# Moving the head-norm sums of the input stage behind the third chunk of a later unit

## The reference, cut to what matters

```python
u = rmsnorm(h, mix_norm[l])
(fq, fk, fv, ff, dq, dk, dv, iq, ik, iw, mq, g) = jnp.split(u @ w_in[l], SPLIT_POINTS, axis=-1)
fq = rmsnorm(fq.reshape(B, S, FOX_HEADS, FOX_HEAD_DIM), fox_q_norm[l])      # fk alike
dq = rope(rmsnorm(dq.reshape(B, S, DSA_HEADS, DSA_HEAD_DIM), dsa_q_norm[l]), cos, sin)   # dk alike
iq = rope(iq.reshape(B, S, IDX_HEADS, IDX_DIM), cos_i, sin_i)               # ik alike, no norm
km = rmsnorm(km.reshape(B, M, MEM_HEADS, MEM_HEAD_DIM), mem_k_norm[l])      # mq alike
gates = jax.nn.sigmoid(g.reshape(B, S, N_BRANCHES, D))
```

## Time and profile before

| what | value |
|---|---|
| timed runs | 1811.56, 1811.9, 1815.14 us (median 1811.9) |
| profiled execution | 1814.24 us, span 1812.4 us |
| PE busy | 1770.3 us, 98% of the span |
| DVE, ACT, POOL busy | 695.6, 695.5, 816.3 us (38%, 38%, 45%) |
| granted PE clock | 0.995 over the span |
| chain that ended last | PE 90%, DVE 6%, ACT 2% |
| from unit 2's products to the scores | 392.88 to 582.58 us after the span's start |

### The profile page before, as it was taken

The page is one execution under the profiler, slowest core; times in us unless marked ns, Lnnn a source line. Parts: engine busy times, 40 slices in busy tenths (PEclk is TensorE's granted clock), DMA queues, the critical chain, the costliest instruction groups (busy, mean ns, idle before and its releaser), DMA issues.

```text
span 1812.4 us, 23268 instructions
## 1 busy us (share of the span) xinstructions
PE 1770.3 (98%) x8458; PEld 1436.1 (79%) x8458; DVE 695.6 (38%) x1129; ACT 695.5 (38%) x1117; POOL 816.3 (45%) x376
## 2 busy tenths in 40 slices
PE   7999999999999999999999999999999999999997
PEld 5888888877887777787878888888866788888886
DVE  4222240068777875235352222200675522222002
ACT  4232222155555477785342223311424432232212
POOL 4444444447565532324544444444533444444442
PEclk9999999999999999999999999999999999999998
DMA  4233232332333221112223223223251222232232
GB/s 159 93 101 96 93 102 96 100 104 84 104 115 111 70 71 48 47 47 76 99 83 103 93 94 103 93 95 102 92 147 59 93 93 93 93 103 93 93 104 70
DMA packets 49342, 168.22 MB, mean 93 GB/s; under 512 B 6008, under 2 KB 6520, under 8 KB 49152
## 3 DMA queue, kind: packets, MB, share of 16 engines
q1 hardware_dynamic: 46368, 161.86, 27.5%
q10 hardware_dynamic: 2912, 5.52, 1.0%
HBM read 161.84 MB, written 2.11 MB: 90 GB/s over the span
## 4 chain that ended last, share of the span: by engine, by line
PE 90%; DVE 6%; ACT 2%; DMA 1%; issue 1%; POOL 0%; SPq 0%; DVEq 0%; ACTq 0%
PE bank L476 25%; PE bank L478 25%; PE bank L477 25%; PE bank L671 8%; DVE input_low L1295 2%; PE bank L716 2%; PE bank L742 2%; PE bank L839 1%; PE bank L733 1%; DVE bank L1431 1%; DMA raw_weights<-weights 1%; DVE residual L1331 1%; PE bank L545 0%; ACT weights_high L939 0%; DMA residual<-x_t 0%
## 5 line engine op out<-in xcount | busy, mean ns | idle before, releaser
L409 POOL TENSOR_TENSOR weights_low<-raw_weights,weights_high 128x1024 fp32r<-128x1024 f32 x296 | 717.7, 2426 | 934.2 <-ACT weights_high L939 933.9
L476 PE MATMUL bank<-input_high,weights_high 128*128 128x512 f32 x1424 | 560.3, 393 | 15.9 <-DVE input_low L1295 15.2
L477 PE MATMUL bank<-input_high,weights_low 128*128 128x512 f32 x1424 | 556.4, 391 | 0.0
L478 PE MATMUL bank<-input_low,weights_high 128*128 128x512 f32 x1424 | 556.1, 391 | 0.0
L939 ACT CAST weights_high<-raw_weights 128x1024 fp32r<-128x1024 f32 x296 | 308.2, 1044 | 307.4 <-DMA raw_weights<-weights 289.9
L476 PEld LDWEIGHTS bank<-input_high,weights_high 128*128 128x128 f32 x1424 | 268.4, 189 | 78.9 <-issue 12.5
L478 PEld LDWEIGHTS bank<-input_low,weights_high 128*128 128x128 f32 x1424 | 268.5, 189 | 56.6
L477 PEld LDWEIGHTS bank<-input_high,weights_low 128*128 128x128 f32 x1424 | 268.7, 189 | 55.0 <-issue 0.2
L478 PE MATMUL bank<-hidden_low,weights_high 128*128 (+1 forms) x528 | 205.5, 389 | 0.0
L476 PE MATMUL bank<-hidden_high,weights_high 128*128 (+1 forms) x528 | 205.5, 389 | 0.0
L477 PE MATMUL bank<-hidden_high,weights_low 128*128 (+1 forms) x528 | 205.5, 389 | 0.0
(11 more groups left out here) (237 smaller groups left out, 1842.1 us busy)
## 6 DMA issues: line engine op xcount, KB each, us to landing
raw_weights<-weights SPq DMA_DIRECT2D x296, 512.0 KB, 3.4
residual<-x_t SPq DMA_DIRECT2D x4, 512.0 KB, 8.1
out_t<-out_t SPq DMA_DIRECT2D x8, 256.0 KB, 2.2
glu_stacked<-glu_padded ACTq DMA_DIRECT2D x24, 64.0 KB, 3.9
glu_stacked<-glu_padded SPq DMA_DIRECT2D x24, 64.0 KB, 3.9
mem_in<-mem_t ACTq DMA_DIRECT2D x1, 1024.0 KB, 4.9
tile<-forget_sums ACTq DMA_DIRECT2D x4, 256.0 KB, 3.4
rope_cos<-forget_sums ACTq DMA_DIRECT2D x2, 256.0 KB, 3.8
```

Source lines behind the costliest of these rows:

```text
L409: pool.tensor_tensor(wl[:, u % RING, :], raw[:, u % RING, :], wh[:, u % RING, :].bitcast(F32), ALU.subtract).then_inc(low_done, 1)
L476: pe.matmul(out, wh[:, u % RING, w], rh, start=start, stop=False)
L477: pe.matmul(out, wl[:, u % RING, w], rh, start=False, stop=False)
L478: return pe.matmul(out, wh[:, u % RING, w], rl, start=False, stop=stop)
```

## The change

PE's sums for unit i move from behind unit i+1 into unit i+2, behind its third chunk (after nine of its 24 matmuls); a helper `head_sums` holds them. In the fills they come behind nine gate products. On ACT the square root for unit j-1 moves behind the forget gates' log and the memory input's work of its step. On DVE the reciprocal moves from the end of step i+1 to step i+2, right before the normalisation and thus behind the take of unit i+2. The wait for the forget gates' sum to be out (`forget_out`) moves from step 6 to step 11. The banks of the first two thirds of `proj` change places for this stage only, and the wait for all takes before the first gate unit is split: 32 takes before gate unit 0, all 34 before gate unit 1.

```diff
-        proj = [bank[0], bank[1], bank[7]]
+        proj, proj2 = [bank[1], bank[0], bank[7]], [bank[0], bank[1], bank[7]]
+        HEAD_SUMS_BEHIND = 2
@@ PE
-            def project(u, out, rh, rl, low_at, n=S):
+            def project(u, out, rh, rl, low_at, n=S, inside=None, behind=None):
                 pe.wait_ge(low_done, low_at)
                 for k in range(DK):
                     mm = products(out, u, k, rh[:, k, 0:n], rl[:, k, 0:n], k == 0, k == DK - 1)
-                mm.then_inc(unit_done, 1)
+                    if k == DK - 1:
+                        mm.then_inc(unit_done, 1)
+                    if k == behind:
+                        inside()
+            def head_sums(i):
+                kind, n = IN_STEPS[i], tokens(IN_STEPS[i])
+                if kind in NORM:
+                    k = upto_step(IN_STEPS, NORM, i)
+                    if k == 1:
+                        pe.wait_ge(sem("ones_rounded"), 2)
+                    pe.wait_ge(sem("in_square_low"), k)
+                    if k > 2:
+                        pe.wait_ge(sem("in_normed"), k - 2)
+                    group = (bd_r if heads(kind) == 2 else ones_r)[:, :]
+                    pe.matmul(norm_banks[k % 2][:, 0:n], group, sq_high[k % 2][:, 0:n], start=True, stop=False)
+                    pe.matmul(norm_banks[k % 2][:, 0:n], group, sq_low[k % 2][:, 0:n], start=False, stop=True
+                              ).then_inc(sem("in_summed"), 1)
...
-                        project(U_IN + j, proj[j % 3][:, 0:n], rh, rl, U_IN + j + 1, n)
+                        project(U_IN + j, proj[j % 3][:, 0:n], rh, rl, U_IN + j + 1, n,
+                                inside=lambda: head_sums(j - 2), behind=HEAD_SUMS_BEHIND)
                     else:
-                        fill(FILLS[j - n_steps])
+                        fill(3 * (HEAD_SUMS_BEHIND + 1))
+                        if j - 2 < n_steps:
+                            head_sums(j - 2)
+                        fill(FILLS[j - n_steps] - 3 * (HEAD_SUMS_BEHIND + 1))
...
-                    if j == 6:
+                    if j == MEM_STEP + 11:
                         pe.wait_ge(sem("forget_out"), 1)
...
-                    if g == 0:
-                        pe.wait_ge(sem("in_taken"), len(IN_STEPS))
+                    if g < 2:
+                        pe.wait_ge(sem("in_taken"), len(IN_STEPS) - 2 * (g == 0))
@@ ACT: this block moves from before the forget gates' log to behind the memory input's work
                     i = j - 1
                     if 0 <= i < n_steps and IN_STEPS[i] in NORM:
...
                         act.wait_ge(sem("in_summed"), k)
                         act.activation(norm_banks[k % 2][:, 0:n], norm_banks[k % 2][:, 0:n], ACT.Sqrt, bias=eps[:, 0:1],
@@ DVE, in the block of i = j - 2
+                        dve.wait_ge(sem("in_rooted"), k)
+                        root_k = norm_banks[k % 2][:, 0:n]
+                        dve.reciprocal(root_k, root_k).then_inc(sem("in_inverse"), 1)
                         dve.wait_ge(sem("in_inverse"), k)
                         dve.scalar_tensor_tensor(out=out, in0=t, scalar=v(gain)[0:m],
...
-                    i = j - 1
-                    if 0 <= i < n_steps and IN_STEPS[i] in NORM:
-                        k, n = upto_step(IN_STEPS, NORM, i), tokens(IN_STEPS[i])
-                        dve.wait_ge(sem("in_rooted"), k)
-                        root_k = norm_banks[k % 2][:, 0:n]
-                        dve.reciprocal(root_k, root_k).then_inc(sem("in_inverse"), 1)
```

More of the change, by code:

```diff
@@ L603, in stepped @@
                         kind, n = IN_STEPS[i], tokens(IN_STEPS[i])
[L604 to L615, removed]
                         if kind in TURN:
@@ L634, in stepped @@
                         mm.then_inc(sem("forget_summed"), 1)
-                    if j == 6:
+                    if j == MEM_STEP + 11:
                         pe.wait_ge(sem("forget_out"), 1)
-                    if j == MEM_STEP + 11:
                         pe.wait_ge(sem("squares_added"), squares("mix") + DK - 1)
@@ L880, in pool_half @@
                         mm.then_inc(unit_done, 1)
-            pair_start("mix2", U_IN2, proj[0][:, :], proj[1][:, :])
+            pair_start("mix2", U_IN2, proj2[0][:, :], proj2[1][:, :])
             for j in range(2, len(IN2_STEPS)):
@@ L888, in _ @@
                     spread_factor("mix2")
-                project(U_IN2 + j, proj[j % 3][:, :], xh, xl, U_IN2 + j + 1)
+                project(U_IN2 + j, proj2[j % 3][:, :], xh, xl, U_IN2 + j + 1)
                 if j in CONV_AFTER:
@@ L1019, in stepped @@
                         feed_root("mem", bank[6], MEM // P)
+                    i = j - 1
+                    if 0 <= i < n_steps and IN_STEPS[i] in NORM:
+                        kind, n = IN_STEPS[i], tokens(IN_STEPS[i])
+                        k = upto_step(IN_STEPS, NORM, i)
+                        act.wait_ge(sem("in_summed"), k)
+                        act.activation(norm_banks[k % 2][:, 0:n], norm_banks[k % 2][:, 0:n], ACT.Sqrt, bias=eps[:, 0:1],
+                                       scale=float(heads(kind)) / P).then_inc(sem("in_rooted"), 1)
                     i = j - 2
@@ L1659, in _ @@
                 dve.wait_ge(unit_done, U_IN2 + j + 1)
-                dve.tensor_tensor(out, proj[j % 3][:, :], rstd[:, :], ALU.mult).then_inc(sem("in2_taken"), 1)
+                dve.tensor_tensor(out, proj2[j % 3][:, :], rstd[:, :], ALU.mult).then_inc(sem("in2_taken"), 1)
                 if kind == "s":
```

## The result

| | before | after |
|---|---|---|
| median of six timed runs | 1812.26 us | 1823.62 us |
| lowest, highest | 1811.56, 1815.14 | 1822.49, 2093.49 |
| profiled execution, span | 1814.24, 1812.4 | 1823.64, 1821.8 |

What follows compares the result with a forecast made beforehand. TensorE, busy 98% of the span, was taken as the bound, so only its gaps count. Three stretches, 1.4 + 6.8 + 1.0 = +9.2 us on a median of 1811.9, gave 1821.1 us, range 1814.5 to 1825.5.

Steps and rivals of the forecast that it cites:

- Free edits, gate unit 0: Before the gate units: swapped banks let gate unit 0 start behind take 31, long done; 0.66 us won.
- the forget wait's removal: Wait for the forget gates' sum, moved to step 11: met 25 us ahead there, so free.
- Stretch A: To the end of unit 10: VectorE and GpSimd alternate, take 4 comes late, VectorE's period stays 6.75; +1.4 us.
- The drain behind a table load: ScalarE's root behind the forget log: the skill's rule would add 1.4 us; the forecast left it out, seeing no drain.
- Stretch B: From the end of unit 10 to the start of unit 29: late normalisation delays rounding and weights; +6.8 us.
- The three waits: TensorE before units 21, 25 and 29 waits 2.2 us each for the weights' low part, 2.3 with restart; 6.9 together.
- the small ones of the first group: Units 12 to 17: three new TensorE waits of 0.8, 0.9 and 1.4 us, two old ones gone; -0.1 together.
- Stretch C: From unit 29 to the scores: VectorE does two reciprocals behind the take of unit 33, TensorE waits 1.7; +1.0 us.
- The faster one: Rival: the later reciprocal is covered, weights come in time and the waits just go; -6.2 us, 1805.7; chance 0.07.
- The rival without VectorE's hold in the first nine steps: GpSimd does not hold VectorE there: -2.9 instead of +1.4 to the end of unit 10; +4.9, 1816.8 us; chance 0.18.
- The heavier rival: VectorE falls further behind: Stretch A at its upper bound, +4.4, groups at 2.7; +13.4, 1825.3 us; chance 0.10.

Runs made afterwards that it cites:

- free parts alone: Kernel before with only the swapped banks, the split gate wait and the forget wait moved to step 11: 1812.22 us, ratio 1.000.
- early memory low part: Changed kernel with VectorE's low part of the memory input moved from the end of its step to right behind the next take: 1821.49 us, ratio 1.0051.
- early rounding: Changed kernel with ScalarE rounding the weights of unit j+3 ahead of the rotation copies instead of behind them: 1811.91 us, ratio 1.0001.
- version of before with the early memory low part: Kernel before plus swapped banks, split gate wait, forget wait in step 11, and VectorE's memory low part behind the take: 1810.26 us, ratio 0.9988.
- root's place: Changed kernel with ScalarE's square root back ahead of the forget gates' log and the memory work: 1823.49 us, ratio 1.0068.

## Why the prediction came out as it did

The direction, the size and the mechanism were right; 1823.6 lies 2.5 above 1821.1 and inside the range. By its steps:

- **Free edits, gate unit 0.** Right: in the free parts alone 0.67 is won from unit 33 to gate unit 1, predicted 0.66; in the change gate unit 0 starts 0.56 earlier, and gate unit 1 then waits for its weights. The prediction gave the forget wait's removal no gain of its own, and alone it has none left at unit 11 (-0.12).
- **Stretch A, +1.4.** Measured +1.42, and also its inner steps: take 4 at 418.51 counted in the frame of before (417.87 + 0.64), predicted 418.5; rotation ends 413.20, 414.34, 416.04, predicted 413.15, 414.3, 416.0; sums of unit 8 at 450.37, predicted 450.3. GpSimd's two small instructions took 1.18 and 1.62 instead of 0.6 and 1.15. Those two sizes were off by 1.05 in all and take 4 by nothing; that the two engines held each other in turn, and so ended where the sum of their work does, is how I read it, not shown by a run. On this the Trainium skill (SBUF — State Buffer, "SBUF: two separate sides") says that of a VectorE instruction with two SBUF inputs and a GpSimd instruction that reads SBUF the one that starts first has the shared port pair for the whole instruction and the other is blocked entirely; the rows above agree, each of VectorE's ends 0.3 to 0.55 behind GpSimd's. The early memory low part, 4.4 us, is its price here.
- **The drain behind a table load.** The trace decides against it once more: by the rule of the Trainium skill (ScalarE: Activation LUTs, What ACT_TABLE_LOAD costs) the root would be 1.38 later. Timeline of ACT after:

```profile
405.26 1.28 ACT L1029 ACT_TABLE_LOAD   x1
406.56 0.66 ACT L1029 ACTIVATE bank<-bank,epsilons 128x512 f32<-128x512 f32 x1
```

- **Stretch B, +6.8.** The three waits are 2.25, 2.31 and 2.24, predicted 2.2; the small ones of the first group are 0.72, 0.87 and 1.16, predicted 0.8, 0.9 and 1.4. That group came to +0.1, predicted -0.1 (from unit 11 to 18 -0.39, and 0.46 of it is the order of the sums). Measured is +8.7 in all. What failed is the sentence that a group costs its wait and a restart: from unit 22 to 26 it cost 2.4, near the predicted 2.3, but from 18 to 22 it cost 3.9. Behind its wait TensorE ran eight matmuls at a distance of 0.427 instead of 0.227, 1.6 us in all. PE's timeline, and the granted clock of the stretch around it (us, then busy time of PE, PEld, DVE, ACT and POOL with their counts, clock, DMA share, GB/s):

```profile
507.89 0.46 PE L477 MATMUL bank<-input_high,weights_high 128*128 128x512 f32 x1 [2.25 <-POOL weights_low L410]
...
509.30 0.63 PE L479 MATMUL bank<-input_low,weights_high 128*128 128x512 f32 x1
509.73 0.63 PE L477 MATMUL bank<-input_high,weights_high 128*128 128x512 f32 x1
```

```profile
508.00:513.00 5.00, 5.00 (x16) 3.96 (x17) 3.47 (x5) 2.09 (x3) 5.00 (x3) 0.66 0.08 34
```

- **Stretch C, +1.0.** The mis-sized term, measured +2.8, above even its upper bound of +2.2. TensorE waits 2.44 for VectorE's chain from the take of unit 33 (580.24) to the end of the mask (594.73): 14.49, predicted 12.8. Of the 1.65 more, 1.55 is the rotation of unit 30, 3.48 instead of 1.93, since GpSimd held its first instruction; the prediction had put this hold only into its bound, and too small, at 1.2. With the early rounding GpSimd's instruction is elsewhere, the rotation takes 1.93, and stretch C is +1.3. Timeline of DVE in that run:

```profile
572.84 0.69 DVE L1438 TENSOR_TENSOR tile<-tile,rope_sin 128x512 f32<-128x512 f32 x1
...
574.77 3.36 DVE L1426 RECIPROCAL bank<-bank 128x512 f32<-128x512 f32 x1
```

  The hold of dk's rotation was not foreseen either. It made the take of unit 32 late (578.10), ScalarE's squares and copies behind it, and the rounding of gate unit 1 behind those (583.08), and TensorE stood 0.69 for it. That adds nothing at the scores: the take of unit 33 waited for TensorE and not for it, and TensorE would have waited for the mask instead.
- **The sum.** +12.94 at the scores against +9.2. That the span differs by 9.4, as if the sum were exact, is partly luck: 3.5 us outside the stage went the other way.
- **The rivals.** The faster one would have needed the weights in time; early rounding made it so, and the time fell by 11.7 against the change. So its place was right and its condition was not met. Its price was not: it had -6.2, and with the weights in time alone the scores are at -0.91. Only with stretch A's hold taken away too do they reach -5.10. The rival without VectorE's hold in the first nine steps fell, and named its price well: with the hold taken away stretch A is -3.02, where it had -2.9. The heavier rival fell as well: stretch A was +1.4 and not +4.4, and a group without the half-clock stretch cost 2.4 and not 2.7.

Open: why half clock comes at all behind one of three almost equal waits. Stretches of 3.41 us lie behind the wait before unit 21 in the change and in the versions with the root or the memory low part moved, at other places of the stage in two more, and in none of the seven others, before among them; no experiment varied the wait alone. No run took the GpSimd hold out of the last steps by itself; early rounding took it out and moved ScalarE's work as well.

## What to carry to other kernels

Before an operation is made later, list what stands behind each instruction that waits for it, in its engine's order: here one rounding, with no data from the normalisation at all, stood behind copies that did, and turned a later reciprocal of 3.4 us, on an engine that is busy 38% of the time, into a wait of 2.2 to 2.3 us on TensorE three times. At these three places either of the two was harmless alone: the old normalisation with the rounding there (the kernel before) and the late one with the rounding ahead (early rounding) had no such wait. Put work that feeds the bound engine ahead of anything that can wait. And look for waits that ask for more than the next instruction needs: splitting the one before the scores moved them by 1.9 us.

## What the runs showed of the hardware

- VectorE's reciprocal of 512 columns in a bank took 3.34 to 3.37 in all twelve traces, beside a GpSimd instruction or not. Its 512-column instructions with two SBUF inputs took 0.67 to 0.70 beside an idle GpSimd and, in the change, up to 2.87 beside a busy one.
- A wait of 2.25 us on TensorE was followed by 3.41 us at a granted clock of 0.5, the level of 1.2 GHz, starting 1.0 us behind the restart; waits of 2.31 and 2.24 us before units 25 and 29 were not. In the version of before with the early memory low part a wait of 1.78 us was followed by such a stretch 0.15 behind its restart; the same wait of 1.78 in before was not.
- Ten of the twelve traces have a half-clock stretch that starts between 816 and 837 us, of 3.41 or 6.83 us; those of the free parts alone and of the root's place have none. Against before, which has the longer one, TensorE comes 1.3 to 1.5 us earlier past it with the shorter one and 2.9 earlier with none, which three rounds can mistake for an effect.
